# First block's mixer: where the weight splits stand on ScalarE and VectorE, and three output tiles begun together

## What is computed

```python
for l in range(DEPTH):                                  # DEPTH = 2
    x = x + 0.5 * swiglu(rmsnorm(x, ffn1_norm[l]), w_ffn1_in[l], w_ffn1_out[l])
    u = rmsnorm(x, mix_norm[l])
    c_q, c_kv, k_r, hq, hf, hi, hgate, mq, gate_logits = split_sizes(u @ w_in[l], IN_SPLITS)
    y_mla = mla_branch(c_q, c_kv, k_r, ...) @ w_o_mla[l]         # 8 heads, causal softmax
    y_hg = hgrn2_branch(hq, hf, hi, hgate, ...) @ w_o_hg[l]      # a gated recurrence
    y_mem = memory_branch(mq, mem_n, w_mem_kv[l]) @ w_o_mem[l]   # 4 heads, softmax
    gates = jax.nn.sigmoid(gate_logits.reshape(B, S, N_BRANCH, D))
    merged = gates[:, :, 0] * y_mla + gates[:, :, 1] * y_hg + gates[:, :, 2] * y_mem
    x = x + merged @ w_out[l]
    x = x + 0.5 * swiglu(rmsnorm(x, ffn2_norm[l]), w_ffn2_in[l], w_ffn2_out[l])
```

## Time and profile before

| | |
|---|---|
| runs (3) | median 2357.98 us, 2355.84 to 2358.05 |
| profiled execution | 2355.99 us, span 2354.2 us |
| TensorE matmul busy | 2333.3 us, 99% of the span |
| VectorE, ScalarE, GpSimd busy | 1639.6, 1277.4, 346.9 us |
| granted TensorE clock | 0.999 mean |

### The profile page before, as it was taken

One profiled execution on the slowest core, in us unless ns is written; L12 is line 12 of the kernel. 1 busy time (PEld: TensorE's weight loads), 2 busy tenths in 40 slices (PEclk: granted clock), 3 DMA queues, 4 the chain that ended last, 5 costly groups with the idle time before them and its releaser, 6 DMA issues.

```text
span 2354.2 us, 50733 instructions
## 1 busy us (share of the span) xinstructions
PE 2333.3 (99%) x21750; PEld 2275.3 (97%) x21750; DVE 1639.6 (70%) x2270; ACT 1277.4 (54%) x1828; POOL 346.9 (15%) x296
## 2 busy tenths in 40 slices
PE   9999999999999999999999999999999999999998
PEld 9999999999999999999999999989999999989998
DVE  7865777966677657878666766776765766776763
ACT  6644656654455456565455554636554554646554
POOL 2012020300200210203003002431002002431001
PEclk9999999999999999999999999999999999999999
DMA  6555533465555545335555645422655545422643
GB/s 255 202 193 194 179 126 126 180 213 182 197 194 190 192 180 185 118 141 183 197 196 181 223 180 197 168 80 91 215 180 197 197 182 196 173 74 92 216 180 124
DMA packets 57680, 410.21 MB, mean 174 GB/s; under 512 B 6384, under 2 KB 6640, under 8 KB 8688
## 3 DMA queue, kind: packets, MB, share of 16 engines
q1 hardware_dynamic: 56448, 401.62, 47.4%
q10 hardware_dynamic: 1008, 5.34, 0.6%
HBM read 405.89 MB, written 1.05 MB: 173 GB/s over the span
## 4 chain that ended last, share of the span: by engine, by line
PE 84%; DVE 7%; ACT 4%; issue 4%; POOL 1%; DMA 0%; DVEq 0%; ACTq 0%; SPq 0%; POOLq 0%
PE bank L558 83%; DVE sb_wlo L514 3%; DVE area L1862 1%; ACT sb_whi L506 1%; PE bank L2210 1%; ACT area L1582 0%; DVE area L1845 0%; DVE area L1811 0%; DVE area L648 0%; POOL sb_x_ssq L701 0%; ACT area L1648 0%; DVE area L1919 0%; ACT area L1606 0%; POOL area L839 0%; ACT area L1603 0%
## 5 line engine op out<-in xcount | busy, mean ns | idle before, releaser
L558 PE MATMUL bank<-area,sb_whi 128*128 128x256 f32 x11752 | 2017.1, 278 | 3.1 <-ACT area L782 1.2
L558 PEld LDWEIGHTS bank<-area,sb_whi 128*128 128x128 f32 x11752 | 1769.1, 188 | 12.6 <-issue 4.2
L558 PE MATMUL bank<-area,sb_wlo 128*128 128x256 f32 x5876 | 1606.4, 277 | 5.2 <-DVE sb_wlo L514 5.0
L506 ACT ACTIVATE sb_whi<-sb_raw 128x1024 fp32r<-128x1024 f32 x762 | 793.0, 1055 | 596.0 <-PE bank L558 582.6
L558 PEld LDWEIGHTS bank<-area,sb_wlo 128*128 128x128 f32 x5876 | 1094.4, 188 | 7.7 <-DVE sb_wlo L514 7.6
L514 DVE TENSOR_TENSOR sb_wlo<-sb_raw,sb_whi 128x1024 fp32r<-128x1024 f32 x762 | 954.7, 1264 | 156.8 <-ACT sb_whi L506 154.9
L648 DVE TENSOR_TENSOR area<-bank,sb_x_diag 128x512 f32<-128x512 f32 x244 | 166.8, 684 | 72.0 <-PE bank L558 49.7
L999 DVE TENSOR_TENSOR area<-area,area 128x256 f32<-128x256 f32 x176 | 76.2, 433 | 186.7 <-ACT area L950 185.5
L558 PE MATMUL bank<-area,area 64*64 64x64 f32 (+5 forms) x2864 | 149.5, 248 | 0.1
L558 PEld LDWEIGHTS bank<-area,area 64*64 64x64 f32 (+3 forms) x2864 | 127.3, 139 | 19.2 <-ACT area L1630 5.3
L693 POOL TENSOR_TENSOR sb_x_ssq<-sb_x 128x256 f32<-128x256 f32 x9 | 12.0, 1331 | 849.3 <-DVE sb_x L1043 839.1
(11 more groups left out here) (272 smaller groups left out, 1148.3 us busy)
## 6 DMA issues: line engine op xcount, KB each, us to landing
sb_raw<-stream SPq DMA_DIRECT2D x379, 1024.0 KB, 4.8
sb_raw<-stream SPq DMA_DIRECT2D x3, 512.0 KB, 7.2
area<-lora ACTq DMA_DIRECT2D x2, 768.0 KB, 6.1
area<-c ACTq DMA_DIRECT2D x1, 1504.0 KB, 7.5
sb_x<-x SPq DMA_DIRECT2D x4, 256.0 KB, 5.4
area<-mem ACTq DMA_DIRECT2D x1, 1024.0 KB, 8.5
out<-sb_x SPq DMA_DIRECT2D x4, 256.0 KB, 2.9
sb_raw<-stream ACTq DMA_DIRECT2D x1, 512.0 KB, 4.8
```

What stands on the lines that cost most here:

```text
L506: e.activation(k.hi[k.slot[p]], raw_piece(k, p), ACT.Copy).then_inc(*k.done("weights_hi", p))
L558: return e.matmul(out, lhsT, rhs, start=start, stop=stop, skip_group_check=True, tile_position=at)
```

## The change

Five things, all in the first block's mixer:

1. In the loop over heads ScalarE makes its two splits ahead of the head's exponentials, in place of after the recurrence's exponentials.
2. In the same loop VectorE makes its two low parts ahead of the recurrence's step, in place of last.
3. The product with `w_out` begins three output tiles together (18 blocks before merged tile 6), and the last splits of the merge move accordingly: one high part goes ahead of merged tiles 6 and 7, and on VectorE both last sums and one low part go ahead of the two remainders.
4. First swap: ScalarE's split of the piece for the latents' values goes ahead of copying the rows of `hg_values`.
5. Second swap: for h = 13 VectorE scales the last pair of gates ahead of the low part of the values.

```diff
-AHEAD1 = (2, (6, 2))
+AHEAD1 = (3, (6, 2))
...
-    hi_parts(e, k, 3 * PIECE)
+    hi_parts(e, k, 4 * PIECE)
     copied_rows(e, k, ("hg_values", s), m.vh, k.sx.tm)
-    hi_parts(e, k, PIECE)
...
         if h < HEADS:
+            hi_parts(e, k, 2 * PIECE)
             scalar_exponentials(e, k, s, m, h)
...
         scalar_recurrence(e, k, s, m, h)
-        if h <= HEADS:
+        if h == HEADS:
             hi_parts(e, k, 2 * PIECE)
-        if h == HEADS:
...
+    hi_parts(e, k, PIECE)
     scalar_merged(e, k, s, m, 6)
     scalar_merged(e, k, s, m, 7)
-    hi_parts(e, k, 2 * PIECE)
+    hi_parts(e, k, (AHEAD1[0] - 1) * PIECE)
     for j in range(NX):
-        if j >= 2:
+        if j >= AHEAD1[0]:
             hi_parts(e, k, PIECE)
...
             vector_softmax(e, k, s, m, h)
+        name, i, dst = fillers[h]
+        if h > HEADS:
+            scaled_pair(e, k, ("projected", s, name, i), dst)
...
-        vector_recurrence(e, k, s, m, l, h)
-        name, i, dst = fillers[h]
-        scaled_pair(e, k, ("projected", s, name, i), dst)
         if h < HEADS:
             lo_parts(e, k, 2 * PIECE)
-        elif h == HEADS:
+        vector_recurrence(e, k, s, m, l, h)
+        if h <= HEADS:
+            scaled_pair(e, k, ("projected", s, name, i), dst)
+        if h == HEADS:
...
-    for j in (6, 7):
-        vector_merged(e, k, s, m, j)
-        vector_merged_lo(e, k, s, m, j)
-    lo_parts(e, k, 2 * PIECE)
+    vector_merged(e, k, s, m, 6)
+    vector_merged(e, k, s, m, 7)
+    lo_parts(e, k, PIECE)
+    vector_merged_lo(e, k, s, m, 6)
+    vector_merged_lo(e, k, s, m, 7)
+    lo_parts(e, k, (AHEAD1[0] - 1) * PIECE)
     for j in range(NX):
+        if j >= AHEAD1[0]:
+            lo_parts(e, k, PIECE)
         if j >= 2:
-            lo_parts(e, k, PIECE)
             x_low(e, k, s, j - 2)
```

## The result

The changed kernel takes 2416.44 us (median of 5 runs, 2414.72 to 2417.88); the kernel before took 2357.98 beside it. The ratio is 1.025, 95% interval 1.0238 to 1.0263: 58 us slower, where 20 were forecast. Of the profiled execution the span is 2413.6 us, against 2354.2.

What follows compares the result with a forecast made beforehand. The prediction took TensorE, busy 99% of the span, as the bound. From the profiled 2355.99 us, 31.0 added and 10.7 gone gave 2376.3; the runs' median standing 2.0 higher made it 2378.3 us, range 2366 to 2393.

Steps and rivals of the forecast that it cites:

- the queue: Loop of heads: exponentials held behind a split waiting for TensorE make TensorE wait, 3.4 us after h = 1, 3, 5, 7; 15.5 a layer.
- the gains: Outside the heads, per layer: 1.34 and 0.96 us from three output tiles, 0.8 and 0.53 from the swaps.
- The 0.6 after h = 2: Even steps of the heads: VectorE's round of 8.5 to 9.0 us against TensorE's 8.5 costs 0.6 us once.
- The late low parts that went: Heads of both layers: with low parts made early none is late, winning 3.4 us over both layers.
- I take the load as moved, not removed.: Heads: GpSimd's two additions of a step slow VectorE's low parts instead of its products, so the sum stays.
- were it gone: Heads: without GpSimd's load on VectorE an odd step would cost 2.3 us instead of 3.4, 5 us less a layer.
- bears it out only in part: VectorE beside GpSimd: the trace supports the skill's whole-instruction lock only partly, L1862 being 0.85 us longer beside an addition of some 1.3.
- The clock, a rival at 0.13: Heads: half clock after each of eight TensorE waits loses 1.7 us more, 14 in all, giving 2392 us; chance 0.13.
- a clock of 1.00 throughout: Expected sign in the profile after: TensorE's granted clock stays full over the whole run, with no half-clock cost.
- the wait goes, 1.34 a layer: Product with w_out: three output tiles begun together remove TensorE's wait for merged tiles 6 and 7, 1.34 us a layer.
- 0.96 of pace: Product with w_out: without the wait, 192 matmuls run 5 ns faster, 91 in 10 us instead of 87, winning 0.96 us a layer.
- 0.53 and 0.8 of swaps: At 412.52 freeing a bank earlier wins 0.53 us; at 282.33 an earlier split for the latents' values wins 0.8; per layer.

Runs made afterwards that it cites:

- experiment 1: The changed kernel with ScalarE's two splits in the heads back behind the recurrence's exponentials: 2366.33 us, ratio 1.0043.
- experiment 5: The changed kernel with only the second split of each step back behind the recurrence's exponentials, the first staying ahead: 2368.24 us, ratio 1.0054.
- experiment 6: The changed kernel with the heads' seed pieces shifted, so that the split waiting for TensorE's first piece falls on even h: 2407.75 us, ratio 1.0221.
- Experiment 8: The changed kernel with GpSimd's two operations of each level cut to one element per partition, exponentials reading with scale 0: 2384.28 us, ratio 1.0117.
- experiment 2: The changed kernel with VectorE's two low parts in the heads back at the end of the step, ScalarE's splits kept ahead: 2384.32 us, ratio 1.0114.
- experiment 3: The changed kernel with each of the three output tiles' banks awaited just before its own first block: 2405.11 us, ratio 1.0206.
- Experiment 4: The kernel before with both swaps and three output tiles, third bank awaited late, the loop of heads as before: 2352.08 us, ratio 0.9982.
- experiment 11: Experiment 4's kernel with the three tiles' blocks in three turns (5, 1, 2) in place of two (6, 2): 2351.89 us, ratio 0.998.
- experiment 10: Experiment 4's kernel with two output tiles begun together and the merge's last splits as before, leaving the swaps alone: 2357.47 us, ratio 0.9999.

## Why the prediction was wrong, and where it was right

The direction and the mechanism were right. The size was off by 39 us of span (2413.6 against 2374.5, the forecast 2376.3 less the 1.8 between an execution's time and its span), and the time lay above the range, which ended at 2393. Two terms that the sum had at nothing failed, the half clock behind the stands (17 us) and the third tile's bank (10 us); the queue and the gains were mis-sized (7 and 4.4). By the steps of the prediction:

**The queue (15.5 us a layer).** Right in kind, shown by experiments 1, 5 and 6. The measured sum is 19 a layer, where 15.5 was forecast. For h = 3, 5 and 7 the stands are 3.62, 3.45 and 3.20 us, with 0.2 of restart and 0.3 at a turn, 3.7 to 4.1, where 3.4 was forecast. For h = 1 it is 1.58 and, in step 2, 3.29, 5.2 with the restarts, where 3.4 was forecast: the low parts of 4.04 us, and TensorE waits for the masked keeping (L1836) behind the product, which the forecast's chain for h = 1 left out. The 0.6 after h = 2 didn't come. 7 us over both layers. The late low parts that went were put at 3.4 us, from 7 waits; the earlier trace rows has 6, so 3.2.

**"I take the load as moved, not removed."** The load moved, as said, but it costs more where it went: the low parts lose 1.6 to 1.8 us to it (3.96 to 4.16 against 2.35), where the products had lost 1.3 (2.64 against 1.36). Experiment 8 gives the bound "were it gone" its number: 1.80 shown for h = 3 and 5 and 1.60 for h = 7, some 2.1 to 2.3 with restart and turn, where the text has 2.3. The Trainium skill (SBUF — State Buffer, "Who interferes with whom") says that the two engines contend for one pair of ports, here since the low parts have two SBUF inputs, and that this is an exclusive lock. The trace agrees. Alone a low part takes about 1.2 us (2.35 for two); here the two took:

```profile
334.04 2.18 DVE L514 TENSOR_TENSOR sb_wlo<-sb_raw,sb_whi 128x1024 fp32r<-128x1024 f32 x1
336.14 2.06 DVE L514 TENSOR_TENSOR sb_wlo<-sb_raw,sb_whi 128x1024 fp32r<-128x1024 f32 x1
```

The ends of the four operations follow each other as if they took turns: GpSimd's first at 335.14, the low part 1.08 later at 336.22, GpSimd's second 0.90 later at 337.12, the low part 1.08 later at 338.20. So each time shown holds the wait for the other engine's operation, GpSimd's 1.84 too. That is what the prediction missed in "bears it out only in part": it set L1862's extra 0.85 against the whole of an addition that had itself waited. In the step of the earlier trace rows L1862 began at 336.70, 0.01 ahead of GpSimd's addition, and took 0.68, while the addition took 1.57; they had not slipped past each other.

**The clock, a rival at 0.13.** This is the largest term. The heads grew by 24.7 + 27.5 = 52.2 us; stands are 38 of it, and the late low parts that went give 3.4 back, so that about 17.6 are half rate; the seven slow stretches, read one by one, are 17.2. The step that failed is that the sum put this at nothing ("a clock of 1.00 throughout"): the argument against it, that turn, scores and the gates keep the engine busy around the stands, didn't hold. The rival's price of 14 is close partly by luck, eight stands at 1.7, where seven cost 1.5 to 2.8 each. Waits of up to 1.8 us left the clock full in the heads but for two places (experiments 1, 2, 5 and 8). Those of 3.2 to 3.6 halved it in seven of eight cases there, those of experiment 3 (2.96 to 3.62) in eight of eight and those of experiment 6 in six of six. The Trainium skill (TensorE: Matmul & The Clock Gate, "What's actually happening") says that idleness throttles the array and that the chip's watch runs free of the program. The first the trace shows. The second would explain why the same stand of 3.3 us left 1.00 behind it in layer 1 and 0.61 in layer 2, and 0.77 behind that of layer 1 in experiment 3; no run here tests it.

**Part 3, "the wait goes, 1.34 a layer".** The step that failed is that only merged tiles 6 and 7 were considered as what the product waits for. The bank of the third tile is awaited by the list at its head, before the first block, and it is freed by VectorE's reading of the merge's last products. That is 3.6 us of stand and 1.4 of half clock a layer, 10 in all, shown by experiment 3. The code could have told it: the diff changes a number, and a line above the loop makes that many waits of it.

**The gains: 0.96 of pace, 0.53 and 0.8 of swaps, and the 1.34.** Experiment 4 has them all without the stands: 3.9 us of 7.3. The pace stayed at 88 matmuls in 10 us; experiment 11 brought 91 by having merged tile 5 needed later, and won nothing by it. The swaps alone gave nothing that can be measured (experiment 10). Terms read from waits were added up as if each were TensorE's to win, while new waits came up at the end of the merge, where VectorE is just in time. In the changed kernel some 4.4 us of the 7.3 are missing, probably in the same way.

The sum: 7 (longer stands) + 17.6 (clock in the heads) + 10 (bank) + 4.4 (gains not had) = 39.0. The last is what is left of the span outside the heads by the other terms, not measured by itself.

## What to carry to other kernels

Before an operation is moved ahead in an engine's queue, look at what it waits for: a wait that cost nothing at the queue's end holds back all that is then behind it, and the low price of the operation itself (1 us) says nothing. Where a forecast makes TensorE stand over 3 us at a time, price the half clock behind each stand as likely, not as a rival; keeping the waits under 2 us, even by splitting them as in experiment 2, saves most of the half clock besides. When a count of things in flight is raised, read every line that makes a list over it, for a resource that is awaited at the head of the loop and used at its end. And a wait removed ahead of an engine that is just in time is worth what that engine lets through, here nothing measurable for two swaps.

## What the hardware showed that I had not expected

- Adding about 30 us of useless matmuls (eight fillings, 3.72 us shown for one) made the kernel 16 us faster, 2416.4 to 2400.3.
- The same stand in the same step (3.29 us in layer 1, 3.28 in layer 2) was followed by a clock of 1.00 once and 0.61 once, in one execution.
- VectorE and GpSimd took turns by whole operations, and the times shown on both sides hold the waits. Two VectorE subtractions of 128x1024 float32 took 3.96 to 4.16 us beside GpSimd's operations and 2.35 without them, while the products of 128x512 that used to stand beside the same operations went from 1.11 and 1.53 to 0.68 each.
